# Moving the rows of activations by 128 bytes within 256, and the rows of weights that TensorE loads beside them

## The reference

```python
hs = concat([meta, x])                                            # (272, 2048)
hs = hs + 0.5 * swiglu(rmsnorm(hs), gate1, up1, down1)            # 2048 -> 5632 -> 2048
u  = rmsnorm(hs) @ w_in + b_in                                    # 2048 -> 5 * 1024: b, c, v, a, g
y_sc = u_b * causal_dwconv(u_c * u_v, conv_sc_w)                  # 3 taps
z    = causal_dwconv(u_a * sigmoid(u_g), conv_cf_w) + conv_cf_b   # 31 taps
hs = hs + concat([y_sc, silu(layernorm(z))]) @ w_out
hs = hs + 0.5 * swiglu(rmsnorm(hs), gate2, up2, down2)
out = rmsnorm(hs)[16:]                                            # meta tokens dropped
```

## Time and profile before

| | |
|---|---|
| median of three runs | 1861.67 us |
| profiled execution, its own time | 1861.53 us |
| its span in the trace | 1859.7 us |
| TensorE busy | 1848.6 us, 99% |
| VectorE busy | 1088.2 us, 59% |
| ScalarE busy | 902.5 us, 49% |
| DMA queue of SyncE, share of 16 engines | 58.3% |
| granted TensorE clock, mean over the span | 0.999 |

### The profile page before, as it was taken

One profiled execution on the slowest core, in us unless ns is written; L12 is line 12 of the kernel. 1 busy time (PEld: TensorE's weight loads), 2 busy tenths in 40 slices (PEclk: granted clock), 3 DMA queues, 4 the chain that ended last, 5 costly groups with the idle time before them and its releaser, 6 DMA issues.

```text
span 1859.7 us, 34886 instructions
## 1 busy us (share of the span) xinstructions
PE 1848.6 (99%) x14425; PEld 1803.6 (97%) x14425; DVE 1088.2 (59%) x1218; ACT 902.5 (49%) x1151; POOL 5.8 (0%) x16
## 2 busy tenths in 40 slices
PE   9999999999999999999999999999999999999998
PEld 9999999999999999999999999999999999988886
DVE  7555555555554544469899887555555555544454
ACT  6433333434343444359888665444444444444443
POOL 1000000000000000000000000000000000000000
PEclk9999999999999999999999999999999999999999
DMA  6655555555555555555555566666666666656664
GB/s 224 192 178 172 180 171 179 172 177 174 176 176 176 180 174 179 180 170 173 182 182 172 179 201 193 196 192 193 193 194 193 195 193 193 214 188 191 193 188 134
DMA packets 283359, 342.29 MB, mean 184 GB/s; under 512 B 10639, under 2 KB 223985, under 8 KB 283152
## 3 DMA queue, kind: packets, MB, share of 16 engines
q1 hardware_dynamic: 282672, 340.44, 58.3%
q10 hardware_dynamic: 320, 0.53, 0.1%
q0 software_dynamic: 288, 0.19, 0.0%
HBM read 339.02 MB, written 2.10 MB: 183 GB/s over the span
## 4 chain that ended last, share of the span: by engine, by line
PE 99%; DVE 1%; ACT 0%; issue 0%; DVEq 0%
PE ps L484 29%; PE ps L482 28%; PE ps L483 28%; PE ps L578 4%; PE ps L576 4%; PE ps L577 4%; PE ps L464 0%; DVE w_flat_lo L889 0%; PE ps L444 0%; PE ps L594 0%; DVE zc L1090 0%; PE ps L601 0%; DVE ln_mu L915 0%; PE ps L498 0%; ACT o_tok L874 0%; DVE res L1004 0%
## 5 line engine op out<-in xcount | busy, mean ns | idle before, releaser
L889 DVE TENSOR_TENSOR w_flat_lo<-raw,w_flat_hi 128x1024 fp32r<-128x1024 f32 x296 | 361.7, 1224 | 325.8 <-ACT w_flat_hi L661 325.7
L661 ACT ACTIVATE w_flat_hi<-raw 128x1024 fp32r<-128x1024 f32 x296 | 313.9, 1061 | 428.0 <-PE ps L484 286.2
L484 PE MATMUL ps<-x_hi,w_rows_lo 128*128 128x272 f32 x1664 | 483.3, 290 | 0.0
L482 PE MATMUL ps<-x_hi,w_rows_hi 128*128 128x272 f32 x1664 | 479.8, 288 | 1.3 <-DVE x_lo L898 1.2
L483 PE MATMUL ps<-x_lo,w_rows_hi 128*128 128x272 f32 x1664 | 472.3, 284 | 0.0
L889 DVE TENSOR_TENSOR w_rows_lo<-raw,w_rows_hi 128x1024 fp32r<-128x1024 f32 x207 | 253.3, 1224 | 238.0 <-ACT w_rows_hi L661 237.3
L482 PE MATMUL ps<-x_hi,w_flat_hi 128*128 128x256 f32 x1408 | 388.7, 276 | 0.1
L483 PE MATMUL ps<-x_lo,w_flat_hi 128*128 128x256 f32 x1408 | 388.6, 276 | 0.0
L484 PE MATMUL ps<-x_hi,w_flat_lo 128*128 128x256 f32 x1408 | 388.6, 276 | 0.0
L661 ACT ACTIVATE w_rows_hi<-raw 128x1024 fp32r<-128x1024 f32 x207 | 218.9, 1059 | 313.8 <-PE ps L484 312.5
L483 PEld LDWEIGHTS ps<-x_lo,w_rows_hi 128*128 128x128 f32 x1664 | 317.5, 191 | 0.0
(11 more groups left out here) (164 smaller groups left out, 2524.0 us busy)
## 6 DMA issues: line engine op xcount, KB each, us to landing
raw<-in_ffn_w_up SPq DMA_DIRECT2D x176, 512.0 KB, 3.5
raw<-in_ffn_w_down SPq DMA_DIRECT2D x176, 512.0 KB, 4.6
raw<-in_ffn_w_gate SPq DMA_DIRECT2D x175, 512.0 KB, 3.5
raw<-in_w_in SPq DMA_DIRECT2D x80, 512.0 KB, 3.5
raw<-in_w_out SPq DMA_DIRECT2D x32, 512.0 KB, 4.8
x_tok<-in_x SPq DMA_DIRECT2D x4, 512.0 KB, 7.7
gain_tok<-in_final_norm SPq DMA_DIRECT2D x1, 1024.0 KB, 5.0
out_y<-o_tok SPq DMA_DIRECT2D x2, 512.0 KB, 2.9
```

Of the source, the lines that this page charges most:

```text
L482: pe.matmul(dst, w_high, act_high, start=first, stop=False)
L484: return pe.matmul(dst, w_low, act_high, start=False, stop=last)
L661: act.activation(w_of[phase][0][s], raw_rows(phase, s), ACT.Copy).then_inc(hi_ready, 1)
L889: dve.tensor_tensor(w_lo, raw_rows(phase, s), w_hi.bitcast(F32), ALU.subtract).then_inc(lo_ready, 1)
```

## The change

All is address and order; no instruction computes anything else.

1. The padding tensor `to_rows` puts `x_region` and `a_region` at 64 instead of 192 modulo 256. A second one, `to_w`, brings the weights' region back to a multiple of 256.
2. `x2_hi`, `x2_lo`, `y_both` and what lies behind it (`mix_at`) and `a2_both` are moved on by 128 bytes within their regions, so they begin at the same place modulo 256 as before (192, 192 and 0).
3. `w_rows` and `w_pairs` stay. The activations of `gu1`, `ag` and `down1` now begin 64 bytes behind their weights, modulo 256, where it was 192.
4. `cv` takes its weights from `w_flat4`: rows of 1024 bytes, all beginning at 0. Its activations begin at 112 + 64*k, so the distance is 112, 176, 240 and 48 for c = 0 to 3.
5. `w_kept` is turned by 128 bytes: in `b` the distance stays 192.
6. In `cv` and `gu2` the eight products of a block go through c for j = 0 and then for j = 1; before they went through j for each c.
7. Before `b` TensorE waits until `block_used` says that all blocks up to the end of `cv` have been used.

```diff
-        sb("to_rows", [P, (192 - nc.sbuf_base) % 256 // 32 * 8])
+        sb("to_rows", [P, (64 - nc.sbuf_base) % 256 // 32 * 8])
...
         gain1 = sb("gain1", [P, KD])
+        sb("to_w", [P, -nc.sbuf_base % 256 // 32 * 8])
...
-        x2_hi = at("x2_hi", x_at + 0, [P, KD, SEQ], F32R)
-        x2_lo = at("x2_lo", x_at + 0 + 4 * KD * SEQ, [P, KD, SEQ], F32R)
+        x2_hi = at("x2_hi", x_at + 128, [P, KD, SEQ], F32R)
+        x2_lo = at("x2_lo", x_at + 128 + 4 * KD * SEQ, [P, KD, SEQ], F32R)
...
-        w_near = weights("w_near", 4, ROW_BLOCK, lambda s: 4 * (T - NEAR))
         w_pairs = weights("w_pairs", 2, BANK + META, lambda s: 128 * (s % 2))
-        w_kept = weights("w_kept", 2, BANK + META, lambda s: 128 * (s % 2) + 4 * META)
+        w_kept = weights("w_kept", 2, BANK + META, lambda s: (128 * (s % 2) + 4 * META + 128) % 256)
...
-        w_of = {"gu1": w_rows, "ag": w_rows, "cv": w_near, "down1": w_pairs, "b": w_kept,
+        w_of = {"gu1": w_rows, "ag": w_rows, "cv": w_flat4, "down1": w_pairs, "b": w_kept,
...
-        a2_both = at("a2_both", a_at + 64, [P, 2, KF, SEQ], F32R)
+        a2_both = at("a2_both", a_at + 192, [P, 2, KF, SEQ], F32R)
...
-        mix_at = a_at + 0
+        mix_at = a_at + 128
...
-                        for j, c in [(j, c) for c in range(4) for j in range(2)]:
+                        for j, c in ([(j, c) for j in range(2) for c in range(4)] if phase in ("cv", "gu2")
+                                     else [(j, c) for c in range(4) for j in range(2)]):
...
             paired("cv", None)
+            pe.wait_ge(block_used, block0["b"])
             for g in range(G_B):
```

More of the change, by code:

```diff
@@ L100, in build @@
         sb("w_region", [P, 2 * RING * BUFFER])
-        assert w_at % 256 == 0 and x_at % 256 == a_at % 256 == 192 and 4 * BUFFER % 256 == 0
+        assert w_at % 256 == 0 and x_at % 256 == a_at % 256 == 64 and 4 * BUFFER % 256 == 0
         sq = sb("sq", [P, 2, T])
```

## The result

The changed kernel takes 1870.36 us (median of five runs, 1870.23 to 1870.68) against 1861.6 before: 0.47% slower, ratio 1.0047 with a 95% interval of 1.0033 to 1.0062. The span of the profiled execution goes from 1859.7 to 1868.4 us, +8.7.

What follows compares the result with a forecast made beforehand. TensorE bounds the kernel: number of matmuls times distance between their starts. Terms -11.0 (gu1, ag), -3.8 (down1), -1.1 (cv) and -1.3 (b, early out_sc) took 1861.5 to 1844.3 us (median 1844.5); 8-in-10 range 1828 to 1869.

Steps and rivals of the forecast that it cites:

- rows at 64: gu1 and ag, 4992 matmuls: distance from 192 to 64 brings 124.8 ns down to 122.6, -11.0 us.
- down1: 2112 matmuls with the same move of rows: half of the way to the best pace, -3.8 us.
- The bounds: Best and worst for the moved rows: -22.0 to +21.0 us in gu1 and ag, -7.6 to +10.6 in down1.
- The best case: Matmuls of 272 columns at 120.4 ns, gu2's time per column scaled to their width; -22.0 us in gu1 and ag.
- The rival of the other side: gu1, ag and down1: 64 is the worse distance, streams of activations and weights meet oftener; +15.8 us, chance 0.17.
- The rival that nothing happens: The 272-column pace does not hang on the distance, rows give 0; total 1859.5 to 1860.5 us, chance 0.20.
- cv: 768 matmuls with plain weights and other order: changing distance meets good and bad ones, a quarter of the best, -1.1 us.
- b: Restart after a wait costing 0.4 us brings b from 117.8 to 113.3 ns, -1.7 us; net with early out_sc -1.3.
- the -0.8: First seven blocks of out_sc, 168 matmuls, inherit b's good pace, 117.9 to 113.3 ns: -0.8 us.
- the 0.8 that I let VectorE take back: Of 2.5 us gained in b and early out_sc, 0.8 comes back as waits for L889 or the layer norm's sum.
- gu2: 4224 matmuls in the new order of j and c meet the same places and stay at 113.3 ns: 0.
- the rest: out_cf, down2, the padding and VectorE's low part of cv keep their place modulo 256: 0.

Runs made afterwards that it cites:

- rows64: Kernel before with only the rows of 272 columns moved to 64 modulo 256; cv and b weights, order and waits as before; 1870.85 us, ratio 1.0050.
- low_on_64: Kernel before with only the low weights of gu1 and ag moved by 64 bytes, high weights and activations unmoved; 1866.99 us.
- cv_plain: Kernel before with only cv's weights taken from w_flat4, old order of j and c; 1860.44 us in one run.
- best: Kernel before with activations at 0, gu1, ag and down1 weights moved by 64, b's weights at distance 192, wait ahead of out_sc; 1859.35 us, ratio 0.9977.

## Why the prediction was wrong

**The step that failed is *rows at 64*, in its sign, and *`down1`* with it.** I set these stages at -11.0 and -3.8 us; they took +5.6 and +4.7. The bounds held (-22.0 to +21.0 and -7.6 to +10.6), the choice inside them did not. It rested on the sentence that 192 was not shown to suit 272 columns. The runs show it to be the lowest of eight distances in both layouts (in `gu1` level with 0), and rows64 shows that the move to 64 alone costs 1.1 ns a matmul in `gu1` and `ag` and 2.2 in `down1`; its neighbour 224 is the highest. Nothing in the trace of before could say that, and a middle of the bounds with no row behind it should have left the likeliest value at no change, with equal chances to both sides.

**The best case was too deep.** 120.4 ns, the width's need by proportion, was no stage's mean in any kernel. With the steps of the rows gone and at the best distance it was 123.3. In no layout tried did `gu2`'s 113.3 at 256 columns scale to 272. The shorter gap that the prediction quotes from the Trainium skill, page "TensorE: Matmul & The Clock Gate", section "Back-to-back issue gap", is given there for an isolated matmul, and that section says that in a stream of weight loads and matmuls both set the spacing; it entered no term of the sum.

**The rival of the other side was the case that came**: 64 is the worse distance, and the same matmuls lose more. Its reason, that streams of activations and weights meet oftener, is not shown (low_on_64). Its price was too high, +15.8 us against +10.2, because the loss was 1.1 ns in `gu1` and 2.2 in `down1` instead of 2.1 and 2.5. The range reached to 1869.0, and 1870.4 lies 1.4 us outside: it had cut that rival's upper part off.

**The rival that nothing happens fell.** It had drawn on the Trainium skill, page "TensorE: Matmul & The Clock Gate", section "Step-by-step: what each phase is for": loading the next weights is said to take nothing from the running matmul's reads. The prediction's inference from it, that no start of a row could matter, does not hold here: the eight distances lie between 124.03 and 126.78 ns in `down1`. Whether the loads take reads from the streams after all, or something else makes the distance count, no run shows.

***`cv`***: right in sign and size, -1.1 expected and -1.2 measured, without the share of the wait (119.2 against 120.8 ns), but in part by luck. The changing distance for which I had set the -1.1 gave 0.4 us in cv_plain; the larger part came with the order of j and c, to which I had given nothing by itself.

***`b`***: the restart did give a better state, at a price of 0.32 us for which I took 0.4. But `b` came to 116.3 ns, not to 113.3: -0.6 us instead of -1.7. Single distances in it show where the rest is. In every block the matmuls of the first row of weights come down from 118 to 113 ns within four and stay there, and those of the second row are back at 118. The 113 return in each of the 16 blocks without another wait, so the better pace of `b` is a pattern that repeats with its rows and not a state that the steps wear down; why the second row lacks it stays open. And `out_sc` inherited nothing: its window before the sum is 117.6 ns again, so the -0.8 did not come, nor the 0.8 that I let VectorE take back. The fast `out_sc` came where it had not been asked for. In the nine kernels in which the distance in `b` is 0, 32, 64, 96, 128 or 224, `out_sc` ran at 113.7 to 114.1 ns before its sum; in the seven with 192 and no wait ahead of `out_sc`, and in the one with 160, at 117.8. So `b`'s layout goes with the pace that `out_sc` begins with, and the change's turn of `w_kept`, which kept 192 in `b`, stood against the gain that I had set for `out_sc`. No run moved `b`'s distance alone. The other way is the wait right ahead of `out_sc` (best). (The prediction points to the earlier trace rows for `b` running into `out_sc` without a gap; those rows show `cv` and `b`. The trace has no gap at the other seam either, 117 and 119 ns.)

***`gu2`*** and the rest: 0, as predicted; 479.49 us in both with the new order of j and c.

## What to carry to other kernels

When TensorE is the bound and "100% busy", divide the window by the count of records and hold it against the pace of a neighbouring stage: 1 ns a matmul is 7 us in the three stages of 272 columns here, and the busy share does not show it. Where a placement modulo 256 bytes is the change, try each distance on the chip for each width and row pitch, since next neighbours were the best and the worst of eight. Repeat a value in a second kernel before a difference of 1 ns is read as the layout's, since one layout can have two paces. Test the parts of such a change apart: `cv`'s weights and order, worth 2 us alone (with what `b` gained behind them), went under in 10 us of loss.

## What the runs showed of the hardware that was not expected

- The time from one matmul of 272 columns to the next follows the distance between their operands' rows modulo 256 bytes. It is the same when both move together by 64 bytes (530.92 us of `gu1` in both kernels), and it differs in steps finer than 64 bytes (192: 124.0, 224: 126.8 ns in `down1`).
- The same instructions at the same addresses have several steady paces. `cv` ran at 119.2 or 120.3 ns, `out_sc` at 113.3 or 117.8, and `ag` of low_on_64 at 125.8 and 124.7. A pace holds for tens of us. A wait that empties TensorE, 0.3 us, can change it, as in `b`, in `out_sc` and in `ag` of low_on_64, and need not: in low_on_64 `out_sc` was still at 117.8 ns behind its first sum and came to 113.3 only behind the second.
- By what the distance comes to cost time stays open. The low weights moved alone settle nothing, since `ag` had the old pace with them in their new place; the table of eight distances fits no rule that I could state.
